# First embedding gate: one 512-column product for the operand's two halves, squares made by ScalarE

## The chip, the cores and the metric

The kernel runs on one core of one Trainium2 chip. The metric is the device time of one execution in microseconds (us); the time of a kernel is the median of several executions. The engines are TensorE (PE, its weight loads PEld), VectorE (DVE), ScalarE (ACT), GpSimd (POOL, hardly used) and SyncE (SP, which issues the weight transfers). In the profile one execution is recorded, L12 means line 12 of the kernel.

## The reference, cut to what matters

Two transformer blocks are computed on 256 positions of width 2048. The second has two layers; behind each mixer stands an embedding gate. The change touches the gate of layer 0, whose result h is normalised into the operand of layer 1 (the MLA mixer).

```python
for i in range(DEPTH_2):
    xn = rms_norm(h, pre_norm[i])
    out = pool_mixer(xn, ...) if i % 2 == 0 else mla_mixer(xn, ...)
    h = h + rms_norm(out, post_norm[i])
    gate = jax.nn.sigmoid(rms_norm(h, ple_norm[i]) @ ple_w_gate[i])
    h = h + (p[i] @ ple_w_proj[i]) * gate
```

## The kernel before, in words

Activations lie transposed: a block is 128 features by T = 256 positions, KD = 16 blocks make the width 2048. A product of float32 numbers is made of three in a reduced format: every weight is split into hi (ScalarE, a copy, L622) and lo (VectorE, raw minus hi, L1307), each activation operand likewise, and hi x hi + hi x lo + lo x hi is summed in PSUM. Weights arrive in slots of 16 tiles of 128x128 (1 MB, RAW, a ring of four); HI and LO have two buffers each, and each slot is split in two halves. ScalarE splits two slots ahead of the one that TensorE works on, and may overwrite a half of HI when TensorE has counted it in `halves_used`. VectorE makes the lo half when ScalarE's hi half is there.

TensorE has two ways to take a slot. `slot` with `mm3` (L2290 to L2292) goes tile by tile, three matmuls of 256 columns each, and waits for the lo half first. `pair_slot` with `mm2` (L2299, L2300) needs the operand's hi and lo side by side in one tile: all sixteen hi tiles meet both in one matmul of 512 columns, the result's two parts lying in columns 0 to 255 and 256 to 511 of the bank, and then the lo tiles run with 256 columns. Most phases use the second way, the second gate (tag 1) among them; the first gate (tag 0) uses the first way.

The gate has 16 slots, one for each block u of the result, but the first four are taken by quads: four banks are filled at once, as the operand becomes ready in parts. Before them VectorE and ScalarE make the operand (gxh, gxl, L1076 and L2026). Then the code runs in turns, one for each slot from 2 on. In a turn ScalarE splits slot u + 2, then, for the blocks of this turn, applies the sigmoid (L1114) to what VectorE evicted. VectorE makes the lo of slot u + 2, then for block o: `evict` (L2080, bank times rs, rs the root of the norm), `finish` of block o - 1 (L2057 times pj, L2059 add to R; for tag 0 also the square into tmpg, L1341, and its sum into ssq, L1343), `next_rest` of block o - 2 (L2066, the lo part of the next layer's operand xm). ScalarE's `gated_hi` (L1138) makes the hi part of xm of block o - 1 when its R is there; it stands in ScalarE's order behind the sigmoid and ahead of the next turn's split. GATE_TURNS lays out the start: turns 5, 6 and 7 have two blocks, turn 4 only block 1 (block 0 is evicted in turn 3); from turn 8 on block u is taken in turn u. Turns 8 to 15 run in a hardware loop, two rounds of four.

sgt has two buffers, for even and odd blocks. The first quad of mla_in, the next phase, writes the four banks that the last gate blocks used: three of its four banks wait until block 14 is evicted, the fourth until block 15 is. Ones times ssq (L2403), early in its second slot, gives the sum of squares of R. The second gate's `evict` has three steps: ScalarE copies columns 256 to 511 (`gate_right`, L1109), VectorE adds columns 0 to 255 (L2072) and multiplies by rs (L2074).

Between engines all order is made by semaphores, and each engine runs its instructions in the order of the code. `reached(kind, name, n)` gives the count that a semaphore has in a phase; SHARED lists how many steps each phase adds.

Of the kernel before, what the change touches and what calls it, by code (L numbers as in the profile page):

```python
# [20 lines left out]
F32R = mybir.dt.float32r  # L21
# [8 lines left out]
KD = D // P  # L30
# [184 lines left out]
def g_slots_ended(n):  # L215
# [11 lines left out]
    "root": [(n, 1) for n in ("n1", "n2", "np", "nf", "post0", "ple0", "m", "q", "kv", "post1", "ple1")],  # L227
    "ssq": [("n1", 2)] + [(n, 1) for n in ("np", "ple0", "ple1")],
    "part": [(n, 5) for n in ("ple0", "ple1")],
    "squares": [("n1", 8), ("n2", 16), ("post0", 16), ("ple0", 4), ("post1", 16), ("ple1", 4)],  # L230
    "steps": [("n2", 16), ("post0", 16), ("m", 32), ("q", 8), ("kv", 8), ("post1", 16)],
}
SHARED["right"] = [("query", 8), ("gate", 16), ("mix", 16), ("up", KF), ("down", 16), ("pool_in", 64), ("group", 16), ("post0", 16), ("mla_in", 14), ("mla_g", 12), ("post1", 16),
                   ("ple1", 16)]
SHARED["whole"] = [("up", KF), ("pool_in", 64), ("group", 16), ("mla_in", 14), ("mla_g", 12), ("ple1", 16)]
SHARED["made"] = [("y", 2), ("n2", 5), ("lat", 2)]
for _k in ("hi", "x"):
    SHARED[_k] = [("x1", 16), ("y", 4), ("n2", 5), ("np", 16), ("ple0", 5), ("m", 16), ("lat", 2), ("ple1", 5)]
# [2 lines left out]
def reached(kind, name, n=0):  # L241

    names = [a for a, _ in SHARED[kind]]
    return sum(c for _, c in SHARED[kind][:names.index(name)]) + n
# [43 lines left out]
def build(nc, A, out):  # L288
    with ExitStack() as ctx:
        sems = {}  # L290

        def sem(name):
            if name not in sems:
                sems[name] = ctx.enter_context(nc.semaphore(name))
            return sems[name]
# [112 lines left out]
        ot = wk("ot", KD * T, 16)  # L408
        pj0 = wk("pj0", KD * T, 32)
        pth0, ptl0, ptr0 = wk("pth0", 2 * T, 48, F32R), wk("ptl0", 2 * T, 50, F32R), wk("ptr0", 2 * T, 52)  # L410
        gxh, gxl = wk("gxh", KD * T, 64, F32R), wk("gxl", KD * T, 80, F32R)
        sgt = [wk("sgt0", T, 54), wk("sgt1", T, 55)]

        nsq = [wk("nsq0", T, 86), wk("nsq1", T, 87)]
# [19 lines left out]
        kn = wk("kn", 16 * T, 80)  # L434
        v2 = wk("v2", 2 * 2048, 0)
        tmpq = wk("tmpq", T, 30)
        tmpg = wk("tmpg", T, 53)
        s_ = [wk("s0", 384, 48), wk("s1", 384, 49.5)]
        p_ = [wk("p0", 384, 51), wk("p1", 384, 52.5), wk("p2", 384, 54)]
        pt = [wk("pt0", 384, 55.5), wk("pt1", 384, 57)]  # L440
# [22 lines left out]
        def v(name, j=0, n=1):  # L463
            return vec[:, bass.ds(VEC[name] + j, n)] if not isinstance(j, int) else \
                vec[:, VEC[name] + j:VEC[name] + j + n]

        def blk(t, j, n=1):
            return t[:, bass.ds(j * T, n * T)] if not isinstance(j, int) else t[:, j * T:(j + n) * T]
# [26 lines left out]
        def gate_bank(u, r):  # L495

            return (5, 6, 7, 2)[u] if isinstance(u, int) and u < 4 else (0, 1, 3, 4)[r]
# [110 lines left out]
        def _(act):  # L608
# [490 lines left out]
            def gate(tag, tail=0):  # L1099
                name = f"plegate{tag}"  # L1100

                def gate_right(u, r):

                    if tag:
                        act.wait_ge(halves_used, 2 * (BASE[name] + 3) + 1 + u // 2 if isinstance(u, int) and u < 4 else
                                    2 * (BASE[name] + u + 1))
                        if not isinstance(u, int) or u >= 2:
                            act.wait_ge(sem("gate1_used"), u)
                        act.activation(sgt[r % 2][:, :], PS[gate_bank(u, r)][:, T:2 * T], ACT.Copy).then_inc(sem("right"), 1)  # L1109

                def gate_sigmoid(u, r):

                    act.wait_ge(evacuated, EVAC[name] + u + 1)
                    act.activation(sgt[r % 2][:, :], sgt[r % 2][:, :], ACT.Sigmoid).then_inc(sem(f"gate{tag}_ready"), 1)  # L1114

                for i, r in turns(act, 16, tail, lead=2):
                    u = 4 * i + r
                    if not isinstance(u, int) or u >= 2:
                        split(name, i, r)
                    if isinstance(u, int) and u == 3:  # L1120
                        gate_right(0, 0)
                        gate_right(1, 1)
                        root(f"ple{tag}", rs[:, :], PS[4][:, 0:T], D)
                        gate_sigmoid(0, 0)
                    for o, x in [(o, o % 4) for o in GATE_TURNS.get(u, ())] if isinstance(u, int) and u < 8 else [(u, r)]:
                        if not isinstance(o, int) or o >= 2:
                            gate_right(o, x)
                        if not isinstance(o, int) or o:
                            gate_sigmoid(o, x)
                            if tag == 0:  # L1130
                                gated_hi(o - 1)
                if tag == 0:
                    gated_hi(KD - 1)

            def gated_hi(u):

                act.wait_ge(sem("gate0_used"), u + 2)
                act.activation(blk(xmh, u), blk(R, u), ACT.Copy, scale=v("pre1", u)).then_inc(sem("operand_hi"), 1)  # L1138

            act.wait_ge(halves_used, 2 * (BASE["pool_out"]))  # L1140
# [154 lines left out]
        def _(dve):  # L1295
# [42 lines left out]
            def accumulate(st, src, tmp, total=ssq):  # L1338

                st.start()  # L1340
                st.done(dve.tensor_tensor(tmp[:, :], src, src, ALU.mult))  # L1341
                st.wait()
                st.done(dve.tensor_tensor(total[:, :], total[:, :], tmp[:, :], ALU.add))  # L1343
# [709 lines left out]
            def gated(tag, pj, tail=0):  # L2053

                def finish(u, b):
                    dve.wait_ge(sem(f"gate{tag}_ready"), u + 1)
                    dve.tensor_tensor(sgt[b][:, :], sgt[b][:, :], blk(pj, u), ALU.mult).then_inc(sem("gate_mult"), 1)  # L2057
                    dve.wait_ge(sem("gate_mult"), u + (KD * tag + 1))
                    dve.tensor_tensor(blk(R, u), blk(R, u), sgt[b][:, :], ALU.add).then_inc(sem(f"gate{tag}_used"), 1)  # L2059
                    if tag == 0:  # L2060
                        dve.wait_ge(sem(f"gate{tag}_used"), u + 2)
                        accumulate(Steps(dve, sem("square_steps"), reached("steps", "m") + 2 * u), blk(R, u), tmpg)

                def next_rest(u):
                    dve.wait_ge(sem("operand_hi"), reached("hi", "m", 1) + u)
                    dve.scalar_tensor_tensor(blk(xml, u), blk(R, u), v("pre1", u), blk(xmh, u).bitcast(F32),  # L2066
                                             ALU.mult, ALU.subtract).then_inc(sem("operand_rest"), 1)

                def evict(u, b, bank):
                    if tag:  # L2070
                        dve.wait_ge(sem("right"), reached("right", "ple1", 1) + u)
                        dve.tensor_tensor(sgt[b][:, :], sgt[b][:, :], PS[bank][:, 0:T], ALU.add).then_inc(sem("whole"), 1)  # L2072
                        dve.wait_ge(sem("whole"), reached("whole", "ple1", 1) + u)
                        dve.tensor_tensor(sgt[b][:, :], sgt[b][:, :], rs[:, :], ALU.mult).then_inc(evacuated, 1)  # L2074
                    else:
                        dve.wait_ge(halves_used, 2 * (BASE["plegate0"] + 3) + 1 + u // 2 if isinstance(u, int) and u < 4 else
                                    2 * (BASE["plegate0"] + u + 1))
                        if not isinstance(u, int) or u >= 2:
                            dve.wait_ge(sem("gate0_used"), u)
                        dve.tensor_tensor(sgt[b][:, :], PS[bank][:, 0:T], rs[:, :], ALU.mult).then_inc(evacuated, 1)  # L2080

                for i, r in turns(dve, 16, tail, lead=2):
                    u = 4 * i + r
                    if not isinstance(u, int) or u >= 2:
                        split(f"plegate{tag}", i, r)
                    if isinstance(u, int) and u == 3:
                        recip(f"ple{tag}", rs[:, :])
                        dve.memset(ssq[:, :], 0.0).then_inc(sem(f"gate{tag}_used"), 1)
                        dve.wait_ge(sem(f"gate{tag}_used"), 1)
                        evict(0, 0, gate_bank(0, 0))  # L2090
                    for o, x in [(o, o % 4) for o in GATE_TURNS.get(u, ())] if isinstance(u, int) and u < 8 else [(u, r)]:
                        if isinstance(o, int) and o == 0:
                            continue
                        evict(o, x % 2, gate_bank(o, x))
                        finish(o - 1, (x + 1) % 2)
                        if tag == 0 and (not isinstance(o, int) or o >= 2):
                            next_rest(o - 2)
                finish(KD - 1, 1)
                if tag == 0:
                    next_rest(KD - 2)  # L2100
                    next_rest(KD - 1)

            p_rest(0, ptr0, pth0, ptl0)
            for s in range(32):
# [177 lines left out]
        def _(pe):  # L2282
# [615 lines left out]
            proj(0, pth0, ptl0, 0)  # L2898
            sum_squares("post0", "steps")
            proj(0, pth0, ptl0, 1)  # L2900
            gate(0, gxh, gxl)


            by_quads("mla_in", [mla_bank(j) for j in range(4)], halves_of(xm, KD),
# [224 lines left out]
```

## Time and profile before

| what | value |
|---|---|
| median of 3 runs | 2628.92 us (2626.74 to 2629.05) |
| the profiled execution | 2626.53 us |
| its span | 2624.7 us |
| mean granted clock of TensorE | 0.993 of full speed |
| TensorE busy / VectorE / ScalarE | 98% / 76% / 50% |
| first gate: first and last matmul | 2056.2 and 2152.4 us |
| VectorE busy in 2088 to 2116, and 2116 to 2152.4 | 25.06 of 28.00, and 32.34 of 36.40 us |
| ScalarE busy in the same | 14.71 and 19.05 us |

The page of the profile gives shares over the whole span; a change inside one stage is read from views of that stage: the chain of work that ended last in it, who waited for whom, and the instructions in order of time. A matmul's duration in the profile includes its latency, since matmuls overlap; what one costs in a row of them is the distance from start to start. The same holds on ScalarE and VectorE to a smaller degree, so here, too, distances of starts are used.

### The profile page before, as it was taken

How to read it: one execution, taken by the hardware profiler on the slowest of the kernel's cores; microseconds unless marked ns; L12 is line 12 of the kernel's file. 1: busy time of each engine (PE TensorE's matmuls, PEld its weight loads, DVE VectorE, ACT ScalarE, POOL GpSimd, SP SyncE). 2: the span in 40 equal slices, each digit the busy share in tenths (PEclk: the TensorE clock that was granted, in tenths of full speed). 3: DMA queues.
4: the chain of work that ended last, by engine and by line, in shares of the span. 5: the costliest groups of instructions: out<-in, count | busy, mean ns of one | idle time of the engine just before them, and what ended most of it. 6: DMA issues, size and time to landing. Idle time of an engine off the chain costs nothing.

```text
span 2624.7 us, 41249 instructions
## 1 busy us (share of the span) xinstructions
PE 2567.7 (98%) x15774; PEld 2229.0 (85%) x15774; DVE 1987.9 (76%) x3108; ACT 1322.2 (50%) x1973; POOL 0.2 (0%) x4
## 2 busy tenths in 40 slices
PE   5999999999899999999999999999999999999999
PEld 2687778888788888888888888888888998988888
DVE  4587888978988888888556777777654889567577
ACT  3334434455555555553444544445444655676564
POOL 0000000000000000000000000000000000000000
PEclk8999999999999999999999999999999999999999
DMA  9876675426555555558555555555555444543543
GB/s 399 357 311 259 242 290 206 147 73 243 189 192 184 185 190 192 187 184 314 190 189 185 194 192 187 184 189 193 195 185 187 171 171 178 195 142 117 194 170 134
DMA packets 114256, 530.36 MB, mean 202 GB/s; under 512 B 8224, under 2 KB 8768, under 8 KB 65232
## 3 DMA queue, kind: packets, MB, share of 16 engines
q1 hardware_dynamic: 110448, 507.54, 53.2%
q10 hardware_dynamic: 3680, 21.05, 2.2%
q8 instruction: 88, 1.44, 0.2%
q14 instruction: 40, 0.33, 0.0%
HBM read 526.46 MB, written 2.10 MB: 201 GB/s over the span
## 4 chain that ended last, share of the span: by engine, by line
PE 71%; DVE 8%; ACT 3%; issue 1%; ACTq 0%; DVEq 0%
PE ps L2299 43%; PE ps L2300 22%; DVE lo L1307 3%; ACT hi L622 1%; PE ps L2292 1%; PE ps L2291 1%; PE ps L2290 1%; PE ps L2736 1%; PE ps L2562 0%; ACT p L1263 0%; DVE R L2020 0%; DVE O L2018 0%; PE ps L2596 0%; PE ps L2599 0%; DVE R L2059 0%
## 5 line engine op out<-in xcount | busy, mean ns | idle before, releaser
L1307 DVE TENSOR_TENSOR lo<-raw,hi 128x1024 fp32r<-128x1024 f32 x700 | 827.8, 1221 | 387.9 <-ACT hi L622 387.6
L622 ACT ACTIVATE hi<-raw 128x1024 fp32r<-128x1024 f32 x700 | 709.2, 1055 | 637.0 <-PE ps L2300 605.2
L2299 PE MATMUL ps<-x,hi 128*128 128x512 f32 x1376 | 330.6, 392 | 4.7 <-DVE x L1813 4.7
L2299 PEld LDWEIGHTS ps<-x,hi 128*128 128x128 f32 x1376 | 253.6, 189 | 54.4 <-issue 4.9
L2299 PE MATMUL ps<-y,hi 128*128 128x512 f32 x1024 | 250.6, 392 | 0.7 <-DVE y L1727 0.6
L2299 PE MATMUL ps<-xp,hi 128*128 128x512 f32 x1024 | 244.7, 391 | 0.1
L646 ACT ACTIVATE hi<-raw 128x1024 fp32r<-128x1024 f32 x98 | 103.0, 1058 | 231.8 <-DMA raw<-in_weights 94.2
L2299 PEld LDWEIGHTS ps<-xp,hi 128*128 128x128 f32 x1024 | 188.2, 188 | 36.7 <-ACT hi L622 0.3
L2299 PEld LDWEIGHTS ps<-y,hi 128*128 128x128 f32 x1024 | 186.1, 189 | 35.6 <-issue 1.0
L2300 PEld LDWEIGHTS ps<-x,lo 128*128 128x128 f32 x1376 | 177.1, 192 | 7.0
L2300 PE MATMUL ps<-x,lo 128*128 128x256 f32 x1376 | 179.1, 283 | 0.0
L2299 PE MATMUL ps<-hx,hi 128*128 128x512 f32 x688 | 164.6, 391 | 0.0
L1372 DVE TENSOR_TENSOR lo<-raw,hi 128x1024 fp32r<-128x1024 f32 x98 | 118.9, 1221 | 57.0 <-ACT hi L646 56.8
L2299 PEld LDWEIGHTS ps<-hx,hi 128*128 128x128 f32 x688 | 126.3, 188 | 24.3
L1405 DVE SCALAR_TENSOR_TENSOR wsum<-raw,csil,wsum 128x512 f32<-128x512 f32 x180 | 135.1, 751 | 9.0 <-DMA raw<-in_weights 3.5
L2300 PEld LDWEIGHTS ps<-y,lo 128*128 128x128 f32 x1024 | 135.5, 191 | 7.5
L2300 PE MATMUL ps<-y,lo 128*128 128x256 f32 x1024 | 137.8, 282 | 0.0
L2300 PEld LDWEIGHTS ps<-xp,lo 128*128 128x128 f32 x1024 | 131.3, 191 | 5.0
L2300 PE MATMUL ps<-xp,lo 128*128 128x256 f32 x1024 | 132.8, 283 | 0.0
L2299 PE MATMUL ps<-xm,hi 128*128 128x512 f32 x416 | 106.2, 397 | 1.1 <-DVE sgt L2080 1.1
L2287 PE MATMUL ps<-hi,xx 128*128 128x512 f32 x256 | 101.2, 395 | 0.0
L2299 PE MATMUL ps<-xx,hi 128*128 128x512 f32 x384 | 99.8, 402 | 0.0
(396 smaller groups left out, 4197.2 us busy)
## 6 DMA issues: line engine op xcount, KB each, us to landing
raw<-in_weights SPq DMA_DIRECT2D x453, 1024.0 KB, 4.8
wlast<-in_weights ACTq DMA_DIRECT2D x16, 1024.0 KB, 6.0
spare<-in_weights SPq DMA_DIRECT2D x13, 1024.0 KB, 22.2
over_squares<-in_weights SPq DMA_DIRECT2D x9, 1024.0 KB, 16.8
xf<-in_xt SPq DMA_DIRECT2D x4, 1024.0 KB, 9.4
raw<-in_weights SPq DMA_DIRECT2D x4, 768.0 KB, 4.3
R<-in_xt ACTq DMA_DIRECT2D x1, 2048.0 KB, 7.3
out<-R SPq DMA_DIRECT2D x1, 1024.0 KB, 8.6
```

Source lines behind the costliest of these rows:

```text
L622: act.activation(HI[p % PAIR][:, c], RAW[p % RING][:, c], ACT.Copy).then_inc(hi_ready, 1)
L646: act.activation(by_outputs(t, half_of(HI, n)), front_raw(t, h * SLOT // 2, SLOT // 2), ACT.Copy).then_inc(hi_ready, 1)
L1307: dve.tensor_tensor(LO[p % PAIR][:, c], RAW[p % RING][:, c], HI[p % PAIR][:, c].bitcast(F32), ALU.subtract).then_inc(lo_ready, 1)
L1372: dve.tensor_tensor(by_outputs(t, half_of(LO, n)), front_raw(t, h * SLOT // 2, SLOT // 2), by_outputs(t, half_of(HI, n)).bitcast(F32), ALU ...
L1405: ins = dve.scalar_tensor_tensor(total[:, :], piece, scale, total[:, :], ALU.mult, ALU.add)
L2287: pe.matmul(o, ah, wh, start=start, stop=False, **kw)
L2290: pe.matmul(o, wh, ah, start=start, stop=False, **kw)
L2291: pe.matmul(o, wh, al, start=False, stop=False, **kw)
L2292: return pe.matmul(o, wl, ah, start=False, stop=stop, **kw)
L2299: return pe.matmul(o, h, pair[:, :, k, :], start=start, stop=False, **kw)
L2300: return pe.matmul(o[:, 0, :], l, pair[:, 0, k, :], start=False, stop=stop, **kw)
L2736: pe.matmul(PS[4 + d][:, j * T:(j + 1) * T], W[:, t * T + j * P:t * T + (j + 1) * P], V[:, vc:vc + DV], start=(j, t) in ((0, 0), (1, 1 if ...
```

## The change

- TensorE runs the first gate with `pair_slot` and `mm2`: gxh and gxl become two halves of one tile gx at the same place, and `gate` is called with it as the pair.
- `gate_right` and the three-step `evict` now hold for both gates, so ScalarE has one more copy for each block, and VectorE two steps where it had one. They count in `right` and `whole`.
- The square of R leaves VectorE. ScalarE makes it in `gated_hi`, ahead of the hi part of xm, into one of two buffers tmpg; VectorE adds it to ssq in `next_rest`, a block later than before. ScalarE waits for a free buffer, VectorE for the square. `steps` of m has 16 counts in place of 32.

```diff
-    "squares": [("n1", 8), ("n2", 16), ("post0", 16), ("ple0", 4), ("post1", 16), ("ple1", 4)],
-    "steps": [("n2", 16), ("post0", 16), ("m", 32), ("q", 8), ("kv", 8), ("post1", 16)],
+    "squares": [("n1", 8), ("n2", 16), ("post0", 16), ("ple0", 4), ("m", 16), ("post1", 16), ("ple1", 4)],
+    "steps": [("n2", 16), ("post0", 16), ("m", 16), ("q", 8), ("kv", 8), ("post1", 16)],
...
-        gxh, gxl = wk("gxh", KD * T, 64, F32R), wk("gxl", KD * T, 80, F32R)
+        gx = wk("gx", 2 * KD * T, 64, F32R)
+        gxh, gxl = gx[:, 0:KD * T], gx[:, KD * T:2 * KD * T]
...
-        tmpg = wk("tmpg", T, 53)
+        tmpg = [wk("tmpg0", T, 52), wk("tmpg1", T, 53)]
...
                 def gate_right(u, r):
 
-                    if tag:
-                        act.wait_ge(halves_used, 2 * (BASE[name] + 3) + 1 + u // 2 if isinstance(u, int) and u < 4 else
-                                    2 * (BASE[name] + u + 1))
-                        if not isinstance(u, int) or u >= 2:
-                            act.wait_ge(sem("gate1_used"), u)
-                        act.activation(sgt[r % 2][:, :], PS[gate_bank(u, r)][:, T:2 * T], ACT.Copy).then_inc(sem("right"), 1)
+                    act.wait_ge(halves_used, 2 * (BASE[name] + 3) + 1 + u // 2 if isinstance(u, int) and u < 4 else
+                                2 * (BASE[name] + u + 1))
+                    if not isinstance(u, int) or u >= 2:
+                        act.wait_ge(sem(f"gate{tag}_used"), u)
+                    act.activation(sgt[r % 2][:, :], PS[gate_bank(u, r)][:, T:2 * T], ACT.Copy).then_inc(sem("right"), 1)
...
-            def gated_hi(u):
+            def gated_hi(u, b):
 
                 act.wait_ge(sem("gate0_used"), u + 2)
+                if not isinstance(u, int) or u >= 2:
+                    act.wait_ge(sem("square_steps"), reached("steps", "m") + u - 1)
+                act.activation(tmpg[b][:, :], blk(R, u), ACT.Square).then_inc(sem("squares_ready"), 1)
                 act.activation(blk(xmh, u), blk(R, u), ACT.Copy, scale=v("pre1", u)).then_inc(sem("operand_hi"), 1)
...
-                    if tag == 0:
-                        dve.wait_ge(sem(f"gate{tag}_used"), u + 2)
-                        accumulate(Steps(dve, sem("square_steps"), reached("steps", "m") + 2 * u), blk(R, u), tmpg)
-
-                def next_rest(u):
+
+                def next_rest(u, b):
+                    dve.wait_ge(sem("squares_ready"), reached("squares", "m", 1) + u)
+                    st = Steps(dve, sem("square_steps"), reached("steps", "m") + u)
+                    st.start()
+                    st.done(dve.tensor_tensor(ssq[:, :], ssq[:, :], tmpg[b][:, :], ALU.add))
                     dve.wait_ge(sem("operand_hi"), reached("hi", "m", 1) + u)
...
                 def evict(u, b, bank):
-                    if tag:
-                        dve.wait_ge(sem("right"), reached("right", "ple1", 1) + u)
-                        dve.tensor_tensor(sgt[b][:, :], sgt[b][:, :], PS[bank][:, 0:T], ALU.add).then_inc(sem("whole"), 1)
-                        dve.wait_ge(sem("whole"), reached("whole", "ple1", 1) + u)
-                        dve.tensor_tensor(sgt[b][:, :], sgt[b][:, :], rs[:, :], ALU.mult).then_inc(evacuated, 1)
-                    else:
-                        dve.wait_ge(halves_used, 2 * (BASE["plegate0"] + 3) + 1 + u // 2 if isinstance(u, int) and u < 4 else
-                                    2 * (BASE["plegate0"] + u + 1))
-                        if not isinstance(u, int) or u >= 2:
-                            dve.wait_ge(sem("gate0_used"), u)
-                        dve.tensor_tensor(sgt[b][:, :], PS[bank][:, 0:T], rs[:, :], ALU.mult).then_inc(evacuated, 1)
+                    dve.wait_ge(sem("right"), reached("right", f"ple{tag}", 1) + u)
+                    dve.tensor_tensor(sgt[b][:, :], sgt[b][:, :], PS[bank][:, 0:T], ALU.add).then_inc(sem("whole"), 1)
+                    dve.wait_ge(sem("whole"), reached("whole", f"ple{tag}", 1) + u)
+                    dve.tensor_tensor(sgt[b][:, :], sgt[b][:, :], rs[:, :], ALU.mult).then_inc(evacuated, 1)
...
-            gate(0, gxh, gxl)
+            gate(0, gxh, gxl, 0, halves_of(gx, KD))
```

## Rows read from the trace of the kernel before

**Rows 1.** The page, part 1: busy time and share of each engine.
```profile
PE 2567.7 (98%) x15774; PEld 2229.0 (85%) x15774; DVE 1987.9 (76%) x3108; ACT 1322.2 (50%) x1973; POOL 0.2 (0%) x4
```
**Rows 2.** Chain of work that ended last, 2086 to 2157.6, shares by line.
```profile
by line: issue 23.9%; DVE lo L1307 23.6%; ACT hi L622 17.7%; DVE R L2059 8.5%; DVE sgt L2080 7.9%; DVE sgt L2057 6.7%; DVE rs L1312 2.3%; DVE xm L2066 2.0%; DVE tmpg L1341 1.8%; PE ps L2299 1.7%; ACTq L1138 1.1%; ACT xm L1138 0.8%; ACTq L62
```
**Rows 3.** TensorE's waits, 2082 to 2160: total us, times, longest.
```profile
PE ps L2299 <- DVE sgt L2080: 1.1, 1, 1.1
PE ps L2290 <- DVE lo L1307: 0.9, 1, 0.9
```
**Rows 4.** Timeline, TensorE: start us, us, instruction, [idle before <- releaser].
```profile
2117.84 0.38 PE L2290 MATMUL ps<-gxh,hi 128*128 128x256 f32 x1 [0.87 <-DVE lo L1307]
...
2152.37 0.28 PE L2292 MATMUL ps<-gxh,lo 128*128 128x256 f32 x1
...
2156.47 1.20 PE L2299 MATMUL ps<-xm,hi 128*128 128x512 f32 x4 [1.07 <-DVE sgt L2080]
...
2165.44 3.82 PE L2299 MATMUL ps<-xm,hi 128*128 128x512 f32 x16
...
2171.01 3.82 PE L2299 MATMUL ps<-xm,hi 128*128 128x512 f32 x16
```
**Rows 5.** Timeline, ScalarE, turns 4 to 15.
```profile
2087.79 0.42 ACT L1114 ACTIVATE sgt<-sgt 128x256 f32<-128x256 f32 x1 [3.03 <-DVE sgt L2080]
2088.11 1.99 ACT L622 ACTIVATE hi<-raw 128x1024 fp32r<-128x1024 f32 x2
...
2108.02 2.00 ACT L622 ACTIVATE hi<-raw 128x1024 fp32r<-128x1024 f32 x2
...
2112.62 0.51 ACT L1138 ACTIVATE xm<-R,vec 128x256 fp32r<-128x256 f32 x1 [0.38 <-DVE R L2059]
...
2115.48 1.99 ACT L622 ACTIVATE hi<-raw 128x1024 fp32r<-128x1024 f32 x2
...
2120.39 0.51 ACT L1138 ACTIVATE xm<-R,vec  x1 [0.68 <-DVE R L2059]
2120.80 1.99 ACT L622 ACTIVATE hi<-raw 128x1024 fp32r<-128x1024 f32 x2
...
2152.64 1.99 ACT L622 ACTIVATE hi<-raw 128x1024 fp32r<-128x1024 f32 x2
```
**Rows 6.** Timeline, VectorE, the same turns.
```profile
2112.16 0.43 DVE L2059 TENSOR_TENSOR R<-R,sgt 128x256 f32<-128x256 f32 x1
...
2113.82 0.42 DVE L2080 TENSOR_TENSOR sgt<-ps,rs 128x256 f32<-128x256 f32 x1
...
2119.17 0.42 DVE L2057 TENSOR_TENSOR sgt<-sgt,pj 128x256 f32<-128x256 f32 x1
2119.71 0.42 DVE L2059 TENSOR_TENSOR R<-R,sgt 128x256 f32 x1
...
2156.00 0.42 DVE L2080 TENSOR_TENSOR sgt<-ps,rs 128x256 f32<-128x256 f32 x1
```
**Rows 7.** Timeline of the second gate, ScalarE and VectorE: its eviction.
```profile
2568.61 0.38 ACT L1109 ACTIVATE sgt<-ps 128x256 f32<-128x256 f32 x1 [0.44 <-DVE R L2059]
...
2569.03 0.42 DVE L2072 TENSOR_TENSOR sgt<-sgt,ps 128x256 f32<-128x256 f32 x1 [0.51 <-ACT sgt L1109]
2569.49 0.42 DVE L2074 TENSOR_TENSOR sgt<-sgt,rs 128x256 f32<-128x256 f32 x1
```
**Rows 8.** First gate matmul; then a window: us, busy times, clock, DMA share, GB/s.
```profile
2056.19 0.36 PE L2290 MATMUL ps<-gxh,hi 128*128 128x256 f32 x1 [1.87 <-DVE gxl L2026]
...
2057.00:2063.00 6.00, 6.00 (x39) 5.84 (x38) 5.97 (x9) 4.55 (x8) 0.00 (x0) 0.72 0.07 11
```
**Rows 9.** Timeline, ScalarE, 540 to 566: table loads near a Sigmoid and a Square.
```profile
544.12 1.28 ACT L856 ACT_TABLE_LOAD   x1
545.41 1.91 ACT L856 ACTIVATE gates<-gates 128x2048 f32<-128x2048 f32 x1
...
547.92 0.59 ACT L859 ACTIVATE osq<-ps 128x512 f32<-128x512 f32 x1
```

More of the change, by code:

```diff
@@ L229 @@
     "part": [(n, 5) for n in ("ple0", "ple1")],
-    "squares": [("n1", 8), ("n2", 16), ("post0", 16), ("ple0", 4), ("post1", 16), ("ple1", 4)],
-    "steps": [("n2", 16), ("post0", 16), ("m", 32), ("q", 8), ("kv", 8), ("post1", 16)],
+    "squares": [("n1", 8), ("n2", 16), ("post0", 16), ("ple0", 4), ("m", 16), ("post1", 16), ("ple1", 4)],
+    "steps": [("n2", 16), ("post0", 16), ("m", 16), ("q", 8), ("kv", 8), ("post1", 16)],
 }
-SHARED["right"] = [("query", 8), ("gate", 16), ("mix", 16), ("up", KF), ("down", 16), ("pool_in", 64), ("group", 16), ("post0", 16), ("mla_in", 14), ("mla_g", 12), ("post1", 16),
+SHARED["right"] = [("query", 8), ("gate", 16), ("mix", 16), ("up", KF), ("down", 16), ("pool_in", 64), ("group", 16), ("post0", 16), ("ple0", 16), ("mla_in", 14), ("mla_g", 12), ("post1", 16),
                    ("ple1", 16)]
-SHARED["whole"] = [("up", KF), ("pool_in", 64), ("group", 16), ("mla_in", 14), ("mla_g", 12), ("ple1", 16)]
+SHARED["whole"] = [("up", KF), ("pool_in", 64), ("group", 16), ("ple0", 16), ("mla_in", 14), ("mla_g", 12), ("ple1", 16)]
 SHARED["made"] = [("y", 2), ("n2", 5), ("lat", 2)]
@@ L1130, in gate @@
                             if tag == 0:
-                                gated_hi(o - 1)
+                                gated_hi(o - 1, (x + 1) % 2)
                 if tag == 0:
-                    gated_hi(KD - 1)
-            def gated_hi(u):
+                    gated_hi(KD - 1, 1)
+            def gated_hi(u, b):
                 act.wait_ge(sem("gate0_used"), u + 2)
+                if not isinstance(u, int) or u >= 2:
+                    act.wait_ge(sem("square_steps"), reached("steps", "m") + u - 1)
+                act.activation(tmpg[b][:, :], blk(R, u), ACT.Square).then_inc(sem("squares_ready"), 1)
                 act.activation(blk(xmh, u), blk(R, u), ACT.Copy, scale=v("pre1", u)).then_inc(sem("operand_hi"), 1)
@@ L2096, in gated @@
                         if tag == 0 and (not isinstance(o, int) or o >= 2):
-                            next_rest(o - 2)
+                            next_rest(o - 2, x % 2)
                 finish(KD - 1, 1)
                 if tag == 0:
-                    next_rest(KD - 2)
-                    next_rest(KD - 1)
+                    next_rest(KD - 2, 0)
+                    next_rest(KD - 1, 1)
             p_rest(0, ptr0, pth0, ptl0)
```

## The prediction

> **What bounds the kernel now.** Over the whole span TensorE is busy 98% of the time, VectorE 76%, ScalarE 50% [rows 1]. That share is an average, so I read the stretch that the change touches, about 2056 to 2163 us, by itself, in this order. First the chain of work that ended last, followed back from 2157.6: it consists of VectorE's splits (lo), ScalarE's splits (hi), R, sgt and issue time, and TensorE has 1.7% of it [rows 2]. Then TensorE's waits in the same stretch: it looks full, yet it waits twice, 0.9 us for a lo and 1.1 us for sgt at line 2080 [rows 3]. The second wait is the one that counts. The first products of mla_in run, then four matmuls start at 2156.47, when the last gate block's bank has been read [rows 4]; that eviction starts at 2156.00 on VectorE [rows 6]. So the end of this stage is set by VectorE and ScalarE handing work to each other turn by turn, and TensorE's 2 us of waiting are all that shows of it. After 2156.5 TensorE runs without a gap and is the bound again, so what the handing to and fro loses is lost from the span.
>
> The turns can be read from ScalarE's hi rows. The stage's first eviction is followed by hi at 2088.11 (turn 4). Turn 7 goes from 2108.02 to 2115.48, 7.46 us (two blocks finished in the turn); turns 8 to 14, in the loop, take (2152.64 - 2115.48)/7 = 5.31 us each [rows 5]. TensorE needs 288 matmuls of 256 columns for six slots, and goes from 2117.84 to 2152.37 in them, 0.120 us each or 5.77 us a slot [rows 4]. One round of a turn is: hi half, lo half and lo half, read the bank, multiply by pj, add to R; then ScalarE's xm (the next layer's operand), and only behind it, in ScalarE's order, the next hi. What VectorE does after R (tmpg, ssq, the rest of xm) lies beside ScalarE's xm and hi and costs nothing.
>
> **The change, part by part.**
> TensorE: a product becomes one 512-column and one 256-column matmul in place of three of 256. The same pair in mla_in takes 2171.01 - 2165.44 = 5.57 us a slot [rows 4]. That is 0.2 us less a slot; for 13 slots 2.6 us, and the 0.87 us stall for lo would go too, since the lo products now come behind the hi products. But none of it is on the chain, because the last eviction isn't waiting for TensorE. I cost it at nothing; if the chain had slack, it would be a gain of 3.4 us. The first four slots start when the operand's parts are ready, and TensorE reached them early (it sat idle 1.87 us before the first [rows 8]), so they give nothing either. A half of HI is now released later, after all hi products; ScalarE's split is then two slots behind TensorE's use and has over 1 us to spare in turns 4 to 7.
>
> Eviction: before, VectorE read the bank and multiplied by rs in one instruction. Now ScalarE copies columns 256 to 511, VectorE adds columns 0 to 255, and only after that add has ended multiplies by rs. The second gate of the kernel does exactly this: from the add to the multiplication is 2569.49 - 2569.03 = 0.46 us [rows 7]. In the loop such a step with a wait on a register takes 0.54 us (2119.17 to 2119.71) [rows 6]; I take 0.55. ScalarE's copy in a single turn comes right behind hi, while VectorE is still at its two lo, and is covered.
>
> Square: it leaves VectorE (tmpg), where it was hidden behind ScalarE's xm, and goes to ScalarE ahead of xm, on the path from R to the next hi. Between two independent instructions of that size ScalarE takes 2088.11 - 2087.79 = 0.32 us [rows 5]; I take 0.33. Its new wait (a free tmpg) is for a step of the turn before and costs only the reading of a register; bounds for that 0 and 0.1 us a turn, as R to xm takes 0.46 us unrolled (2112.16 to 2112.62) and 0.68 us in the loop (2119.71 to 2120.39) [rows 5, 6]. Queued behind the Square on ScalarE are xm, the next copy, and the next hi, for which VectorE's lo and, two slots later, TensorE wait.
>
> Two-block turns (5, 6, 7): here ScalarE's copy for the second block stands behind Square and xm. From R to the second bank read was 2113.82 - 2112.16 = 1.66 us [rows 6]. Now it is R to Square 0.46, Square to xm 0.33, xm to copy 0.41 (as xm to hi, 2120.39 to 2120.80 [rows 5]), copy to add 0.42 (2568.61 to 2569.03 [rows 7]), in sum 1.62 us. So the copy takes the place of VectorE's tmpg, ssq and rest, at 0.04 us less.
>
> The sum on the chain: first eviction 0.46; turn 4: 0.46 + 0.33 = 0.79; turns 5 to 7: 3 x (2 x 0.46 + 0.33 - 0.04) = 3.63; turns 8 to 14: 7 x (0.55 + 0.33) = 6.16; last eviction 0.55. Together 11.6 us. Loop turns would be 6.19 us, longer than TensorE's 5.57. Bounds: with 0.46 and 0.33 everywhere 10.9; with 0.1 more in each loop turn and 0.2 in each two-block turn 12.9. The tail (R 15, Square, xm, ssq, the column sums) keeps about the distance to the resumed matmuls that it had; nothing new there.
>
> Clock: TensorE will now run dry. Slot 4 begins about 2082.1, so slot 9 could at 2109.9, but its first hi half is ready 1.05 us into turn 7, at 2108.02 + 0.46 + 0.79 + 2 x 1.21 + 1.05 = 2112.7; in the same way slot 10 waits until 2121.4 in place of 2118.3. Later turns cost it 0.6 us each. An eviction ends 2156.42 - 2152.64 = 3.78 us after its turn begins [rows 5, 6], now 4.33, so block 14's is over at 2161.8, while slot 15 ends at 2157.9: a wait of 3.9 us. Twelve products follow, 2.7 us, and then the wait for block 15's, until 2168.0, 3.5 us. After the idle 1.87 us at 2056.19 the trace shows a granted clock of 0.72 over the 6 us from 2057 [rows 8], thus 28% of 6 us, 1.7 us, lost, part of it at 1.2 GHz. In slots 9 and 10 such a loss is covered, as TensorE then waits for the chain; after the resumption it is paid. Bounds 0 and 3.4 us (twice that row); I take 1.0, since part of it falls into the second wait. Forecast: 11.6 + 1.0 = 12.6 us more.
>
> A rule that speaks against the change harder: a Square between Sigmoids might make ScalarE change its function tables. The trace shows a Sigmoid (L856, 545.41) and then a Square (L859, 547.92) with no table load between [rows 9]. The Trainium skill, ScalarE: Activation LUTs, section on table sets, names relu, copy, identity and abs as the fillers that every set has, and does not name square; taken strictly, each block would need two loads. By that rule the case D below would hold; the row speaks against it.
>
> **Rivals.** A, the forecast. B, TensorE is the bound all the same (the handing has slack that I don't see): the gain is the 3.4 us above, time 2625.5. For it speaks that TensorE waits for only 2 us here [rows 3]; against it, the chain and the 1.1 us wait at the end. It decides if a loop turn stays under 5.57 us. C, the Square is hidden (ScalarE's free time takes it up, so only the eviction's second step counts): 11.6 less 0.33 x 11 turns = 8.0, time 2637. Against it: the hi stands behind it in one queue. D, tables: two loads of 1.28 us [rows 9] for each of 16 blocks, 41 us on top of A, 2682. E, the clock stays at 1.2 GHz through several turns: a slot then takes about twice 5.57 = 11 us, and TensorE becomes the bound of the stage; some 5 to 20 us more than A, 2650 or above. Against it: TensorE is busy 5.6 of 6.2 us in a turn. F, the change does not do as it says, and the time stays: nothing in the diff suggests it.
>
> **How the numbers follow.** The profiled execution took 2626.53 us with a span of 2624.7; with 12.6 it would be 2639.1. The median of the runs is 2628.92, 2.4 higher, which gives 2641.5. I forecast 2641. Chances: A 0.83, B 0.03, C 0.05, D 0.03, E 0.04, F 0.02. A alone reaches from 10.9 on the low execution (2637.5) to 12.9 + 3.4 on the median (2645.2); with C below it and a smaller loss of unknown kind I give 2634.5 to 2646.5. A measurement of this kernel can tell about 0.2%, 5.3 us, from no change. Faster by more 0.02 (B is mostly within that bound), within 0.2%: 0.05, slower 0.93.
>
> **What would show it.** In the profile after: loop turns of 6.1 to 6.3 us from hi to hi (5.31 before), turns 5 to 7 of 8.6 to 8.8 us; TensorE waiting for ScalarE's hi in slots 9 to 15 and for sgt at the multiplication by rs, 3 us and more; its idle time between 2100 and 2170 at some 16 us (2 of before, 12 more, and its own 0.2 us a slot); the resumption of mla_in near 2168 in place of 2156.47; no table load between Sigmoids; xm's first products in at most a short stretch at 1.2 GHz. Wrong would be: loop turns at 5.6 us (B), 5.9 us (C), table loads (D), a clock well under 1 over the stage (E), or a span that gives the 12 us back later, in a wait of mla_in that I have not seen.

## The result: 10 us slower, all of it in the hand-over of the first gate

The changed kernel takes 2638.76 us (median of 6 runs, 2636.83 to 2639.5) against 2628.8 us before (6 runs): 1.004 times as long, 95% interval 1.003 to 1.005. A second set of runs gave 2638.71 against 2627.35, ratio 1.0041 (1.0027 to 1.0055). The profiled execution of the first set has a span of 2637.6 us; mean granted clock 0.991.

The page of after shows how little a page says here. This is its first part, with every engine within one per cent of the share that it had:

```profile
PE 2569.7 (97%) x15518; PEld 2217.9 (84%) x15518; DVE 1986.6 (75%) x3108; ACT 1331.1 (50%) x2005; POOL 0.2 (0%) x4
```

256 matmuls are gone (15774 before, [rows 1]), 32 ScalarE instructions have come (1973 before), and the number of VectorE's is the same. Nothing in it is 10 us. The waits of TensorE between 2040 and 2190 tell more (total us, times, longest):

```profile
PE ps L2296 <- DVE sgt L2077: 8.1, 3, 3.6
PE ps L2296 <- DVE gx L2029: 2.6, 3, 1.9
PE ps L2296 <- ACT hi L623: 2.4, 7, 1.0
```

Before, TensorE waited 1.1 us for an eviction and 0.9 us for a lo [rows 3]; now it waits 8.1 us for evictions (L2077, the multiplication by rs) and 2.4 us for hi. The same in order of time, TensorE's rows that answer to [rows 4]:

```profile
2058.47 0.70 PE L2296 MATMUL ps<-gx,hi 128*128 128x512 f32 x2 [1.87 <-DVE gx L2029]
...
2109.60 5.52 PE L2296 MATMUL ps<-gx,hi 128*128 128x512 f32 x16 [2.83 <-DVE sgt L2077]
...
2123.54 3.94 PE L2296 MATMUL ps<-gx,hi 128*128 128x512 f32 x16 [0.95 <-ACT hi L623]
...
2129.58 3.93 PE L2296 MATMUL ps<-gx,hi 128*128 128x512 f32 x16 [0.19 <-ACT hi L623]
...
2163.39 4.19 PE L2296 MATMUL ps<-xm,hi 128*128 128x512 f32 x12 [3.56 <-DVE sgt L2077]
2169.33 1.19 PE L2296 MATMUL ps<-xm,hi 128*128 128x512 f32 x4 [1.75 <-DVE sgt L2077]
```

Two profiled executions have different starts behind them, so each stage is measured from its own first matmul. Before: 2056.19 [rows 8] to the resumption at 2156.47 [rows 4], 100.3 us. After: 2058.47 to 2169.33, 110.9 us. That is 10.6 us more. From the resumption to the end of the span it is 2624.7 - 2156.5 = 468.2 before and 2637.6 - 2169.3 = 468.3 after: nothing is given back and nothing more is lost. The 2.3 us by which the stage starts later in this execution belong to the execution: the runs of this case that share all code ahead of the gate start it between 2055.7 and 2059.3. In the second profile of the changed kernel it starts at 2056.95 and again takes 110.9 us.

ScalarE's hi rows of after, as [rows 5], one at the start of each turn:

```profile
2090.85 2.00 ACT L623 ACTIVATE hi<-raw 128x1024 fp32r<-128x1024 f32 x2
...
2096.63 1.99 ACT L623 ACTIVATE hi<-raw 128x1024 fp32r<-128x1024 f32 x2
...
2122.45 1.99 ACT L623 ACTIVATE hi<-raw 128x1024 fp32r<-128x1024 f32 x2
...
2165.06 1.99 ACT L623 ACTIVATE hi<-raw 128x1024 fp32r<-128x1024 f32 x2
```

Turn 4 is 5.78 us (5.01 before), turns 5 to 7 are (2122.45 - 2096.63)/3 = 8.61 us each (7.46 before [rows 5]), turns 8 to 14 are (2165.06 - 2122.45)/7 = 6.09 us each (5.31 before [rows 5]). The first loop turn on VectorE, and the hand-over on ScalarE at its end:

```profile
2125.80 0.41 DVE L2075 TENSOR_TENSOR sgt<-sgt,ps 128x256 f32<-128x256 f32 x1
2126.24 0.42 DVE L2077 TENSOR_TENSOR sgt<-sgt,rs 128x256 f32<-128x256 f32 x1
2126.59 0.42 DVE L2060 TENSOR_TENSOR sgt<-sgt,pj 128x256 f32<-128x256 f32 x1
2127.13 0.43 DVE L2062 TENSOR_TENSOR R<-R,sgt 128x256 f32 x1
...
2127.77 0.42 ACT L1140 ACTIVATE tmpg<-R 128x256 f32 x1 [0.65 <-DVE R L2062]
2128.09 0.49 ACT L1141 ACTIVATE xm<-R,vec  x1
2128.49 2.00 ACT L623 ACTIVATE hi<-raw 128x1024 fp32r<-128x1024 f32 x2
```

Two steps are new on the path: from the add to the multiplication 0.44 us, and from Square (L1140) to xm 0.32 us. Everything else has nearly its old distance: R to ScalarE's first instruction 0.64 (0.68 before), xm to hi 0.40 (0.41 before) [rows 5, 6].

One view seems to speak against this reading. The chain that ended last, followed back from 2170.2 in after, has 19% of TensorE in it, where before it had 1.7% [rows 2]. Its shares, and two of its pieces:

```profile
by line: issue 21.3%; PE ps L2296 15.6%; ACT hi L623 15.0%; DVE lo L1310 12.6%; DVE sgt L2075 6.3%; DVE R L2062 5.4%; DVE sgt L2060 5.0%; DVE sgt L2077 4.9%; ACT xm L1141 4.2%; PE ps L2297 3.5%; DVE rs L1315 2.0%; ACT sgt L1109 1.0%; ACT tm
...
2127.48 0.97 PE ps L2297 x8
...
2128.49 1.05 ACT hi L623
```

The view ties the hi at 2128.49 to the half that TensorE gave back at 2128.45, the event that came last. But that hi is for slot 11, and by the code it needs only the halves of slot 9, whose last products began at 2120.51. It started 0.40 us behind xm, as in every turn. So the release didn't hold it up; the experiments below, which move or add instructions of ScalarE alone, say the same.

### The profile page after: what moved, and what is told of

It reads as the page before. It is cut to its first block, busy times and chain, and to the rows that moved or that the text cites. A ratio compares the mean times of both kernels' runs of the same rounds, so it can differ in the third digit from the quotient of the medians.

```text
span 2637.6 us, 40793 instructions
## 1 busy us (share of the span) xinstructions
PE 2569.7 (97%) x15518; PEld 2217.9 (84%) x15518; DVE 1986.6 (75%) x3108; ACT 1331.1 (50%) x2005; POOL 0.2 (0%) x4
## 4 chain that ended last, share of the span: by engine, by line
PE 71%; DVE 7%; ACT 4%; issue 2%; ACTq 0%; DVEq 0%
PE ps L2296 43%; PE ps L2297 22%; DVE lo L1310 2%; ACT hi L623 1%; PE ps L2289 1%; PE ps L2288 1%; PE ps L2287 1%; PE ps L2733 1%; PE ps L2559 0%; ACT p L1266 0%; DVE R L2023 0%; DVE O L2021 0%; PE ps L2593 0%; PE ps L2596 0%; DVE rs L1315 0%
## 5 line engine op out<-in xcount | busy, mean ns | idle before, releaser
L2284 PE MATMUL ps<-hi,xx 128*128 128x512 f32 x256 | 101.7, 397 | 0.0
L2286 PE MATMUL ps<-hi,xx 128*128 128x512 f32 x256 | 100.4, 392 | 0.0
```

Of the source, the lines that this page charges most:

```text
L2284: pe.matmul(o, ah, wh, start=start, stop=False, **kw)
L2286: return pe.matmul(o, al, wh, start=False, stop=stop, **kw)
```

## The experiments

Theory A: the stage ends when VectorE and ScalarE have handed work to each other through all turns; what stands on that path costs its full time, what stands beside it costs nothing, and TensorE's own speed doesn't count. Its rivals are that TensorE is the bound (B), that ScalarE's free time covers the Square (C), and, added here, that it is the amount of work of an engine that costs, not its place. "Before" stands for the kernel before, run in the same rounds. "The stage" is the time from the gate's first matmul to the resumption of mla_in in the profiled execution: 100.3 us before, 110.9 us after.

**Only the pair and the eviction.** The square goes back to VectorE.

```diff
# against the changed kernel
-                act.activation(tmpg[b][:, :], blk(R, u), ACT.Square).then_inc(sem("squares_ready"), 1)
...
+                    if tag == 0:
+                        dve.wait_ge(sem(f"gate{tag}_used"), u + 2)
+                        accumulate(Steps(dve, sem("square_steps"), reached("steps", "m") + 2 * u), blk(R, u), tmpg[1])
```

> The changed kernel with the square back on VectorE (tmpg and ssq behind R, as before), so only the 512-column products and the eviction in three steps are new. Theory A (the stage ends with the hand-over of VectorE and ScalarE): against the kernel before, first eviction 0.46, turn 4 0.46, turns 5 to 7 0.9 each (from R to the second bank read VectorE's own work, 1.66 us, is again longer than ScalarE's 1.3), turns 8 to 14 0.45 each, last eviction 0.45: 7.2 us, time 2636.0, loop turns of 5.76 us. Theory B (TensorE bounds the stage): 3.4 us less than before, 2625.4. If the Square alone made the loss, the time would be that of the kernel before, 2628.8.

Measured: 2636.46 us against 2628.48, ratio 1.003 (1.002 to 1.004). Eight of the ten us are there with no Square on ScalarE. In its trace turn 4 takes 5.48 us, turns 5 to 7 take 8.37 each, loop turns mostly 5.77, and the stage 107.8 us, 7.6 more than before (theory A had 7.2). The first loop turn, from hi to hi:

```profile
2121.49 1.99 ACT L623 ACTIVATE hi<-raw 128x1024 fp32r<-128x1024 f32 x2
...
2127.27 1.99 ACT L623 ACTIVATE hi<-raw 128x1024 fp32r<-128x1024 f32 x2
```

TensorE, with the cheaper products, waits 6.6 us for evictions. Theory B would have made it faster than before.

**Only the square.** The kernel before, with Square on ScalarE in two buffers and its sum in `next_rest`, nothing else.

```diff
# against the kernel before
+                act.activation(tmpg[b][:, :], blk(R, u), ACT.Square).then_inc(sem("squares_ready"), 1)
                 act.activation(blk(xmh, u), blk(R, u), ACT.Copy, scale=v("pre1", u)).then_inc(sem("operand_hi"), 1)
...
-                        accumulate(Steps(dve, sem("square_steps"), reached("steps", "m") + 2 * u), blk(R, u), tmpg)
```

> The kernel before with only the square moved to ScalarE; products by three of 256 columns, eviction in one step. Theory A: turn 4 0.33 more, turns 8 to 14 0.33 each, but in turns 5 to 7 VectorE reaches the second bank 0.58 us sooner (no tmpg, shorter steps) and pays 0.33 at the turn's end, 0.25 less each: in sum 1.9 us more, 2630.7, loop turns of 5.64 us. Theory C (the Square is covered by ScalarE's free time): loop turns stay at 5.31 us, and the time is at or a little under 2628.8.

Measured: 2630.64 us against 2628.48, ratio 1.001 (1.0001 to 1.0019). Its hi rows:

```profile
2092.95 1.99 ACT L622 ACTIVATE hi<-raw 128x1024 fp32r<-128x1024 f32 x2
2100.13 1.99 ACT L622 ACTIVATE hi<-raw 128x1024 fp32r<-128x1024 f32 x2
...
2120.06 1.99 ACT L622 ACTIVATE hi<-raw 128x1024 fp32r<-128x1024 f32 x2
2125.64 1.99 ACT L622 ACTIVATE hi<-raw 128x1024 fp32r<-128x1024 f32 x2
```

A two-block turn is 7.18 us, 0.28 shorter than before (VectorE reaches the second bank sooner), a loop turn 5.58, 0.27 longer. So the Square costs in single turns, against theory C, and gains a little in double ones. The two halves of the change add to 8.0 + 2.2 = 10.2 us by medians, and the whole measured 10.0; that this fits so well is in part luck. In the traces the stage grows by 7.6 and 1.4 us, 9.0 in sum, and by 10.6 with both: the two parts act on each other in the two-block turns, which change by +0.91 and -0.28 us alone and by +1.15 us together. With three-step evictions ScalarE's copy for the second block stands behind the Square, and the gain is lost.

**Both kernels with the order on ScalarE changed.** Square and xm are made a block later, behind the next turn's hi and bank copy. Instructions and counts stay.

```diff
# against the changed kernel; in the kernel before gated_hi has no second argument
                             gate_right(o, x)
+                            if tag == 0:
+                                gated_hi(o - 2, x % 2)
                         if not isinstance(o, int) or o:
                             gate_sigmoid(o, x)
-                            if tag == 0:
-                                gated_hi(o - 1, (x + 1) % 2)
                 if tag == 0:
+                    gated_hi(KD - 2, 0)
                     gated_hi(KD - 1, 1)
```

> The changed kernel with one thing moved: ScalarE makes Square and xm of block u - 2 behind the next turn's hi and its bank copy, in place of those of block u - 1 ahead of the hi. Same instructions, same counts. Theory A: the hand-over becomes hi, lo, add, multiply, sigmoid, 4.6 us a single turn and 6.9 us a two-block turn, under TensorE's 5.57 a slot; TensorE becomes the bound from slot 4 on, no wait for an eviction at mla_in: 15 us less than the changed kernel, 2623.5 (5 less than before). If the loss of the change were in the matmuls, or in VectorE's amount of work, it would stay at 2638.8.

Measured: 2623.68 us against 2628.48 for before, ratio 0.9983 (0.9974 to 0.9992); 15 us less than the changed kernel.

> The kernel before with the same move (xm of block u - 2 behind the next hi). Theory A: it was already nearly at TensorE's pace of 5.77 us a slot, so only its two waits go, 0.9 and 1.1 us: 2626.9. The difference to the changed kernel with the move, some 3.4 us, is then what the 512-column products are worth once TensorE is the bound. Rival: the 512-column products are worth nothing in any case, and both are at the same time.

Measured: 2626.88 us against the same 2628.48, ratio 0.9991 (0.9982 to 1.0): a gain of 1.6 us, at the edge of what these runs can tell; in its trace TensorE no longer waits for a lo or an eviction. In the changed kernel with the move, ScalarE's rows around a turn, and TensorE's rows at the end of the stage, are:

```profile
2116.11 1.99 ACT L623 ACTIVATE hi<-raw 128x1024 fp32r<-128x1024 f32 x2
2118.00 0.36 ACT L1109 ACTIVATE sgt<-ps 128x256 f32<-128x256 f32 x1
2118.26 0.41 ACT L1141 ACTIVATE tmpg<-R 128x256 f32 x1
2118.57 0.50 ACT L1142 ACTIVATE xm<-R,vec  x1
2120.37 0.42 ACT L1114 ACTIVATE sgt<-sgt 128x256 f32<-128x256 f32 x1 [1.30 <-DVE sgt L2078]
2120.69 1.99 ACT L623 ACTIVATE hi<-raw 128x1024 fp32r<-128x1024 f32 x2
```

```profile
2106.66 3.92 PE L2297 MATMUL ps<-gx,hi 128*128 128x512 f32 x16
...
2145.73 3.82 PE L2297 MATMUL ps<-gx,hi 128*128 128x512 f32 x16
2149.38 2.08 PE L2298 MATMUL ps<-gx,lo 128*128 128x256 f32 x16
2151.30 2.91 PE L2297 MATMUL ps<-xm,hi 128*128 128x512 f32 x12
2154.83 1.20 PE L2297 MATMUL ps<-xm,hi 128*128 128x512 f32 x4 [0.63 <-DVE sgt L2078]
```

The first loop turn is 4.58 us now, Square and xm lie in ScalarE's wait for VectorE, and the hi follows the sigmoid. ScalarE and VectorE run ahead, until in the last two turns ScalarE's hi waits for TensorE (0.66 and 0.87 us): TensorE is the bound here. It goes without a wait from slot 8 at 2106.66 to slot 15 at 2145.73, 5.58 us a slot; 0.63 us are left of 8.1 and 2.4. Only here are the 512-column products worth something: the two reordered kernels differ by 3.2 us by medians. The same instructions on the same engines, in another order, make 2623.7 us or 2638.8.

**The changed kernel again, and a Square more.** These four shared the runs of before, 2627.35 us.

> The changed kernel once more, as the measure for the three beside it: 2638.8 as before, some 10 above the kernel before. Loop turns of 6.03 us in every theory.

Measured: 2638.71 us.

> The changed kernel with a second Square of the same size behind each first one on ScalarE, on the path between R and the next hi (its result goes to a free place and is not used). Theory A: 0.31 to 0.33 us more in turn 4, twice that in turns 5 to 7, once in turns 8 to 14: 14 x 0.32 = 4.5 us, 2643.3. If ScalarE's free time covers a Square there (theory C), no change.

```diff
# against the changed kernel
                 act.activation(tmpg[b][:, :], blk(R, u), ACT.Square).then_inc(sem("squares_ready"), 1)
+                act.activation(blk(O, u), blk(R, u), ACT.Square)
```

Measured: 2643.2 us (2642.0 to 2643.56), 4.5 us above the changed kernel beside it (2636.6 to 2639.23). Its loop turn on ScalarE, as answer to the one of after shown above:

```profile
2130.07 0.42 ACT L1140 ACTIVATE tmpg<-R 128x256 f32 x1 [0.64 <-DVE R L2063]
2130.39 0.40 ACT L1141 ACTIVATE O<-R  x1
2130.70 0.49 ACT L1142 ACTIVATE xm<-R,vec  x1
2131.10 1.99 ACT L623 ACTIVATE hi<-raw 128x1024 fp32r<-128x1024 f32 x2
```

Each extra Square pushes xm and hi back by 0.31 us, and a loop turn takes 6.34 us in place of 6.03.

> The same fourteen-odd extra Squares, but issued behind ScalarE's bank copy, where it waits 2 us (0.9 us in the second half of a two-block turn) for VectorE's eviction. Theory A: covered, the time of the changed kernel, 2638.8. If it were ScalarE's amount of work that costs, it would be as slow as with the Squares on the path, 2643.3.

```diff
# against the changed kernel
                             gate_right(o, x)
+                            if tag == 0:
+                                act.activation(blk(O, o - 2), blk(R, o - 2), ACT.Square)
```

Measured: 2637.85 us (2637.21 to 2639.5), no more than the changed kernel. Here the extra Square stands in ScalarE's wait for VectorE, which shrinks from 2.00 to 1.69 us:

```profile
2122.53 0.36 ACT L1109 ACTIVATE sgt<-ps 128x256 f32<-128x256 f32 x1
2122.79 0.41 ACT L1129 ACTIVATE O<-R  x1
2124.89 0.42 ACT L1114 ACTIVATE sgt<-sgt 128x256 f32<-128x256 f32 x1 [1.69 <-DVE sgt L2079]
```

It is the place of the Square that costs, not ScalarE's work.

> The changed kernel with Square and xm exchanged on ScalarE (xm first). Theory A: the next hi stands behind both in either order, so nothing changes, 2638.8 within 1 us. Rival: the loss is that xm comes later, and it would shrink by about a third, to 2635.

The edit exchanges the lines of Square and xm in `gated_hi`. Measured: 2638.99 us (2637.32 to 2639.83), as the changed kernel. In its trace most loop turns are 6.13 to 6.15 us, 0.1 longer than in the changed kernel (the first instruction behind R starts 0.73 us after it in place of 0.64), though xm now comes first; the medians can't tell that much. The delay of xm, VectorE's operand, isn't what costs; the delay of the hi behind both is.

**TensorE a third lighter.**

```diff
# against the kernel before; the products of the first four slots are changed likewise
+                    if phase == "plegate0":
+                        kw = dict(skip_group_check=True)
+                        pe.matmul(PS[bank][:, 0:T], h, blk(ah, n), start=n == 0, stop=False, **kw)
+                        return pe.matmul(PS[bank][:, 0:T], l, blk(ah, n), start=False, stop=n == 15, **kw)
                     return mm3(PS[bank][:, 0:T], h, l, blk(ah, n), blk(al, n), n == 0, n == 15)
```

> The kernel before with TensorE's work in the first gate cut by a third: the product of hi weights and gxl is left out (the second of three matmuls, 256 in all), so the gate is computed from a coarser operand. Nothing else is changed. Theory A (the end of the stage is set by VectorE's and ScalarE's hand-over): the time stays, 2628.5, at most 0.3 less; TensorE only waits more, for lo and for the last eviction, and a stretch at 1.2 GHz after such a wait may add up to 1.7 us. Theory B (TensorE bounds the stage): 256 x 0.12 = 31 us less, 2598.

Measured: 2628.8 us against 2627.95, ratio 1.0001 (0.9992 to 1.0011). 256 matmuls less in a stage where TensorE was busy nearly all the time, and no gain. From 2089 to 2156 TensorE is busy 50.78 of 67.00 us, where it was busy 65.53 before, and the stage takes what it took, 100.3 us. Its two ends, and TensorE's waits from 2054 to 2190:

```profile
2059.26 0.36 PE L2888 MATMUL ps<-gxh,hi 128*128 128x256 f32 x1 [1.87 <-DVE gxl L2026]
...
2159.53 1.19 PE L2299 MATMUL ps<-xm,hi 128*128 128x512 f32 x4 [0.82 <-DVE sgt L2080]
```

```profile
PE ps L2888 <- DVE gxl L2026: 9.2, 5, 2.7
PE ps L2358 <- DVE lo L1307: 8.6, 7, 3.1
PE ps L2358 <- DVE sgt L2080: 4.9, 1, 4.9
PE ps L2299 <- DVE sgt L2080: 3.6, 2, 2.8
```

What was taken from the matmuls came back as waiting; the turns stay at 5.31 us (2123.88 to 2129.18 to 2134.47 in its hi rows) and 7.46 us. This is the plainest evidence that the chain, not TensorE, set the end of the stage already before the change.

## Why the prediction was right, point by point

The bound. Said: VectorE and ScalarE set the end of the stage, TensorE's faster products are worth nothing. Shown by the lighter TensorE (no change), by the pair alone (8 us slower), and by the new order on ScalarE, which alone takes 15 us off.

The terms on the path, forecast and measured in the profile of after:

| term | forecast, us | measured, us |
|---|---|---|
| first eviction to hi | 0.46 | 2090.85 - 2089.61 = 1.24, before 2088.11 - 2087.33 = 0.78: 0.46 |
| turn 4 | 0.79 | 5.78 - 5.01 = 0.77 |
| turns 5 to 7 | 3.63 | 25.82 - 22.36 = 3.46 |
| turns 8 to 14 | 6.16 | 42.61 - 37.16 = 5.45 |
| turn 15 to the last eviction's end | 0.55 | 4.22 - 3.78 = 0.44 |
| clock | 1.0 | 0 |
| sum | 12.6 | 10.6 |

The mechanism was right, three sizes were off. First, the step from add to multiplication in the loop: I took 0.55, the pace of the step from pj to R there; it is 0.44, as unrolled, while the step from pj to R still takes 0.54 (2126.59 to 2127.13). So not every step with a wait on a register is slower in the loop; why the one to R is, no run isolates. Over eight such steps the difference is 0.9 us. Against that, one loop turn, the second, took 6.32 us in place of 6.03 in the profile of after and of its repetition, its Square starting 0.92 us after ScalarE was free, with VectorE's ssq named as the last releaser; the kernels with a Square more, on the path or aside, have no such turn. Why is left open. Second, the two-block turns: the sequence R to second add was forecast at 1.62 and took 2102.80 - 2101.22 = 1.58. Third, the clock: TensorE did fall to 1.2 GHz twice after a wait, in slot 8 (granted clock 0.50 from 2110.6 to 2113.6; its sixteen hi products took 5.36 us to the first lo product, 3.65 at full clock) and in the first twelve products of mla_in (0.50 from 2165 to 2168). But behind the first stretch TensorE still had to wait for ScalarE's hi (0.95 us at slot 10), behind the second for VectorE's eviction (1.75 us), and from the resumption at 2169.3 on the granted clock is 1.00. So the path doesn't hold either stretch, and they cost nothing; the lower end of my bounds was the value.

Where TensorE would wait: the forecast named slot 9, about 3 us for a hi. It waited 2.83 us at slot 8, for the eviction of block 4, whose bank slot 8 writes. The step that failed is that I followed only the hi for each slot and not the bank. It cost nothing in the sum, since this wait is covered like the other. The first wait for a hi came at slot 10, 0.95 us, where I had 3.1. The two waits at mla_in came, 3.56 and 1.75 us in place of 3.9 and 3.5; the second is shorter mostly because the twelve products took 4.19 us, part of them at the lower clock (2.91 in the reordered kernel). In all TensorE's waits in the stage from 2100 on are 10.3 us, where "What would show it" had some 16: the stage grew by 2 us less, and slower products filled about 3 us.

The function tables: the trace of after still has two table loads at the sigmoid's line (2086.2 and 2567.1 us), one for each gate, as before, and none between the Squares and Sigmoids of the stage. The rule of the Trainium skill (ScalarE: Activation LUTs, table sets), read so that Square is not in every set, asks for loads that the trace does not have; the row of the earlier Sigmoid and Square [rows 9] was the better guide.

The rest: 10.6 us in the trace and 10.0 by medians, forecast 12.6, so the forecast was high by a fifth to a quarter, all three misses to the same side. The time behind the resumption stayed the same to 0.1 us.

## What to carry to other kernels

An engine that shows 98% busy need not be the bound of a stage: here the stage's end waited for others. Read what ends the last wait, then count the steps on that path and multiply by the turns. When two engines hand work to each other through in-order queues, ask of every instruction what stands behind it in its queue: work that feeds a later turn belongs behind the one that the other engine is waiting for. Moved there, it was free in this kernel, and only then were the faster products worth their time (3.2 us).

## What the runs showed of the hardware that I had not expected

A drop of TensorE to 1.2 GHz (granted clock 0.94 over 2088 to 2116, 0.90 over 2152.4 to 2169 in the profile of after) cost nothing, as behind each low stretch TensorE still had to wait, 0.95 us for ScalarE's hi and 1.75 us for VectorE's eviction. And the loop on ScalarE and VectorE doesn't make all its steps slower: in the profile of after it adds 0.09 us at the addition to R, about 0.2 us from R to ScalarE's next instruction, and nothing between add and multiplication.
